# Two blocks of a transformer on one core: the mixers' gates as twelve-bit parts, each half unit a group

## The reference

```
def token_mix(x, w_in, ...):
    (sgu_u, sgu_v, ret_q, ret_k, ret_v, ret_g, pool_in,
     c_q, c_kv, k_rope, gate_logits) = _split(x @ w_in, IN_SIZES)
    ys = (sgu_mixer(...), retention_mixer(...), pool_mixer(...), mla_mixer(...))
    gates = jax.nn.sigmoid(gate_logits).reshape(bsz, seq, N_BRANCH, dm)
    merged = gates[:, :, 0] * (ys[0] @ w_branch[0])
    for n in range(1, N_BRANCH):
        merged = merged + gates[:, :, n] * (ys[n] @ w_branch[n])
    return merged @ w_out

for i in range(DEPTH):
    x = layer_norm(ALPHA * x + 0.5 * swiglu(x, ffn1_up[i], ffn1_down[i]), ...)
    x = layer_norm(ALPHA * x + token_mix(x, w_in[i], ...), ...)
    ple = jax.nn.sigmoid(x @ w_ple_gate[i]) * (p[i] @ w_ple[i])
    x = layer_norm(ALPHA * x + 0.5 * swiglu(x, ffn2_up[i], ffn2_down[i]) + ple, ...)
```

## Time and profile before

| | us |
|---|---|
| runs shown: median (of 3) | 2652.66 |
| lowest, highest | 2650.13, 2652.67 |
| profiled execution, its own time | 2655.03 |
| its span on the core | 2653.3 |
| gate stage of layer 1: first gate unit to first merge product | 277.55 to 411.34, 133.8 |
| the same in layer 2 | 987.28 to 1121.08, 133.8 |

### The profile page before, as it was taken

The page is one execution under the profiler, slowest core; times in us unless marked ns, Lnnn a source line. Parts: engine busy times, 40 slices in busy tenths (PEclk is TensorE's granted clock), DMA queues, the critical chain, the costliest instruction groups (busy, mean ns, idle before and its releaser), DMA issues.

```text
span 2653.3 us, 37978 instructions
## 1 busy us (share of the span) xinstructions
PE 2622.0 (99%) x15353; PEld 1913.9 (72%) x15353; DVE 1117.3 (42%) x1589; ACT 676.8 (26%) x1202; POOL 73.5 (3%) x95
## 2 busy tenths in 40 slices
PE   9999999999999999999999999999999999999998
PEld 9989888999999998899989888843333333333333
DVE  6866424686586563157832143321212212112212
ACT  4414220442243142213412043021212121112111
POOL 0010200000000120000001000000000000000000
PEclk9999999999999999999999999999999999999999
DMA  6685334456655843334562644699999999999999
GB/s 233 212 283 187 110 134 153 143 174 229 215 190 190 291 153 127 127 143 159 177 213 90 229 149 158 263 370 426 427 427 428 428 427 428 428 427 428 428 427 400
DMA packets 265652, 705.31 MB, mean 266 GB/s; under 512 B 13124, under 2 KB 155408, under 8 KB 215760
## 3 DMA queue, kind: packets, MB, share of 16 engines
q1 hardware_dynamic: 253520, 663.66, 64.8%
q0 software_dynamic: 9856, 36.41, 3.9%
q10 hardware_dynamic: 2176, 3.83, 0.4%
HBM read 699.61 MB, written 6.60 MB: 266 GB/s over the span
## 4 chain that ended last, share of the span: by engine, by line
PE 84%; DMA 8%; SPq 6%; DVE 1%; issue 1%; ACT 0%; DVEq 0%; ACTq 0%
PE acc L993 12%; PE acc L1090 11%; PE acc L1712 10%; PE acc L1047 6%; PE mix L1051 6%; PE acc L1049 6%; PE acc L1727 5%; SPq L875 4%; PE acc L1532 4%; PE mix L1041 4%; DMA big<-in_w 3%; PE acc L1019 3%; PE acc L1324 2%; SPq L878 2%; PE mix L1700 2%; PE acc L1585 2%
## 5 line engine op out<-in xcount | busy, mean ns | idle before, releaser
L1047 PE MATMUL acc<-branch_parts,area_parts 128*128 128x256 f32 x1176 | 343.9, 292 | 0.2
L1051 PE MATMUL mix<-big_parts,zz_parts 128*128 128x256 f32 x1176 | 332.8, 283 | 0.0
L1049 PE MATMUL acc<-area_parts,ring_parts 128*128 128x256 f32 x1176 | 332.4, 283 | 0.0
L1090 PE MATMUL acc<-big,ring 128*128 128x256 f32 (+1 forms) x1408 | 269.7, 353 | 0.0
L1090 PEld LDWEIGHTS acc<-big,ring 128*128 128x128 f32 x1408 | 241.1, 190 | 28.3 <-issue 0.8
L3027 DVE COPY zz<-acc 128x512 f32<-128x512 f32 x32 | 22.1, 692 | 546.4 <-PE acc L1712 546.4
L1047 PEld LDWEIGHTS acc<-branch_parts,area_parts 128*128 128x128 f32 x1176 | 225.0, 191 | 9.5 <-DVE zz_parts L2369 1.0
L1049 PEld LDWEIGHTS acc<-area_parts,ring_parts 128*128 128x128 f32 x1176 | 225.1, 191 | 0.2
L1051 PEld LDWEIGHTS mix<-big_parts,zz_parts 128*128 128x128 f32 x1176 | 225.0, 191 | 0.0
L993 PE MATMUL acc<-x,ring 128*128 128x256 f32 x1024 | 224.3, 380 | 0.0
L993 PEld LDWEIGHTS acc<-x,ring 128*128 128x128 f32 x1024 | 193.8, 190 | 26.7 <-issue 0.3
(11 more groups left out here) (522 smaller groups left out, 3841.6 us busy)
## 6 DMA issues: line engine op xcount, KB each, us to landing
ring<-in_ffn_up SPq DMA_DIRECT2D x86, 1024.0 KB, 5.0
big<-in_w SPq DMA_DIRECT2D x79, 1024.0 KB, 25.7
ring<-in_w SPq DMA_DIRECT2D x76, 1024.0 KB, 26.0
ring<-in_w_in SPq DMA_DIRECT2D x72, 1024.0 KB, 7.0
area<-in_w SPq DMA_DIRECT2D x57, 1024.0 KB, 26.4
spare<-in_w SPq DMA_DIRECT2D x38, 1024.0 KB, 25.7
area<-in_w_ada POOLq DMA_DIRECT2D x24, 1024.0 KB, 8.5
ring<-in_ffn_down SPq DMA_DIRECT2D x28, 768.0 KB, 4.7
```

The lines of the kernel that those rows point to most:

```text
L1047: pe.matmul(abank(a, b)[:, ts], wg[:, b, k, c * P:c * P + P], xg[:, k, :], start=c == 0 and k == 0, stop=False, skip_group_check=True)
L1049: pe.matmul(abank(a, b)[:, ts], wl[:, k, c0:c0 + P], xl[:, k, :], start=False, stop=k == K - 1, skip_group_check=True)
L1051: mm = pe.matmul(kbank(a, b)[:, ts], wk[:, b, k, c * P:c * P + P], xk[:, k, :], start=False, stop=k == K - 1, skip_group_check=True)
L1090: mm = pe.matmul(outs[c], w[:, k, c * P:c * P + P], rhs(kk), start=opens[c] and kk == 0, stop=kk == FC - 1, skip_group_check=not all(opens))
```

## The change

All eight gate units are now in parts. TensorE's list has `gate_product` for each in the place of `product` and of the last `split_product`: for each half unit (256 columns) a group of its own, whose two `acc` banks hold the g and l products (bank 0) and the K sum with the two plain chunks (bank 1). So the gates no longer use `mix`, and there are 8 more groups in a layer. ScalarE has `gate_sum` (copy the K sum to the gate's place in `big`, then `upper` for the same half of the next unit) and `gate` (sigmoid in place) per half; VectorE has `gate_join` (add the other bank, free the pair, then `lower` for the same half of the next unit).
The parts of x stay in `res` and `tn` up to the last gate unit; for this P transposed (`pT`) goes to `area`, and the weights' parts to the upper end of `area` and, for the last units, to places there that the steps are done with. The rotation of retention's q and k moves from step 0 (`m_stats`) to step 4 (`m_values`), with its VectorE work. The merge gets waits for the sigmoids of units 6 and 7. Counts of the semaphores follow.

```
+        gate_wg, gate_wk = (area_parts[:, c:c + IN].rearrange("p (b k c) -> p b k c", b=2, c=256) for c in (AREA + 2 * T, 5632))
+        def weight_parts(s, n):
+            if s < 2 or n < 4:
+                return PARTS[s][1:3]
+            return gate_wg, (PARTS[2][2] if n < 9 else gate_wk)
+        def gate_group(g, b):
+            return G_GATE + 2 * g + b
...
+            def gate_product(L, g):
+                r, n = GATE + g, 4 + g
...
+                unit_landed(pe, L, r)
+                for b in range(2):
+                    a = gate_group(g, b)
+                    group_open(pe, L, a)
+                    for c in range(2):
+                        c0 = (2 * b + c) * P
+                        for k in range(K, DC):
+                            pe.matmul(abank(a, 1)[:, c * T:c * T + T], w[:, k, c0:c0 + P], x[:, k, :], ...)
+                    pe.wait_ge(k_ready, half_parts(L, 2, n, b))
+                    for c in range(2):
+                        for k in range(K):
+                            pe.matmul(abank(a, 0)[:, ts], wg[:, b, k, c * P:c * P + P], xg[:, k, :], ...)
+                            ml = pe.matmul(abank(a, 0)[:, ts], wl[:, k, c0:c0 + P], xl[:, k, :], ...)
+                            mk = pe.matmul(abank(a, 1)[:, ts], wk[:, b, k, c * P:c * P + P], xk[:, k, :], ...)
+                    ml.then_inc(acc_done, 1)
+                    mk.then_inc(acc_done, 1)
...
                 for n in range(8):
-                    if n:
-                        product(L, GATE + n, G_GATE + n, xs, cols)
-                    else:
-                        split_product(L, 2, 4)
+                    gate_product(L, n)
                     steps[n](L)
...
-            def gate(L, n):
-                a = G_GATE + n
-                for b in range(2):
-                    bank_done(act, L, a, b)
-                    g = act.activation(big[:, 4 * n + 2 * b:4 * n + 2 * b + 2, :],
-                                       abank(a, b).rearrange("p (c t) -> p c t", c=2), ACT.Sigmoid)
-                g.then_inc(acc_free[a % 2], 1)
+            def gate_sum(L, g, b):
+                bank_done(act, L, gate_group(g, b), 1)
+                copy(gate_place(g, b), abank(gate_group(g, b), 1)...).then_inc(k_summed, 1)
+                if g < 7:
+                    upper(L, 2, 5 + g, b)
+            def gate(L, g, b):
+                act.wait_ge(a_joined, 38 * L + 11 + 2 * g + b + 1)
+                return act.activation(gate_place(g, b), gate_place(g, b), ACT.Sigmoid)
...
+            def gate_join(L, g, b):
+                a = gate_group(g, b)
+                bank_done(v, L, a, 1)
+                v.wait_ge(k_summed, sums_made(L, 2) + 6 + 2 * g + b + 1)
+                v.scalar_tensor_tensor(out=gate_place(g, b), in0=pair(abank(a, 0)), scalar=1.0 + 1.0 / STEP, in1=gate_place(g, b),
+                                       op0=ALU.mult, op1=ALU.add).then_inc(acc_free[a % 2], 1)
+                v.drain().then_inc(a_joined, 1)
+                if g < 7:
+                    lower(L, 2, 5 + g, b)
...
                 def merge(n, halves=(0, 1)):
                     br = ORDER[n]
+                    if n in (0, 2):
+                        v.wait_ge(silu_ready, 24 * L + (12, 13)[n // 2])
```

More of the change, by code:

```diff
@@ L235, in mixed_blocks @@
         tables = sb("tables", [P, 2048])
-        area_parts = over("area_parts", [P, 3, SPLIT, 256])
+        area_parts = over("area_parts", [P, WHOLE])
         area = sb("area", [P, WHOLE])
@@ L264, in mixed_blocks @@
         vz = carve(2, 2, T)
+        pT = shaped(area[:, 512:2048], (3, 512))
         vn = carve(2, T)
@@ L835, in _ @@
                 for n in range(8):
-                    banks(L, 2 * (G_PROJ + 3 + n) if n < 2 else 2 * (G_GATE + n - 1))
+                    banks(L, 2 * (G_PROJ + 3 + n) if n < 2 else 2 * gate_group(n - 1, 0))
                     square(L, w_in, GATE + n, MAIN + UC * n)
@@ L1210, in m_values @@
                 pe.wait_ge(rv_ready, L + 1)
+                pe.wait_ge(proj_qk, L + 1)
+                pe.matmul(mix[:, 1, :], const("rot_ret"), rq.rearrange("p c t -> p (c t)"), start=True, stop=True)
+                pe.matmul(mix[:, 2, :], const("rot_ret"), rk.rearrange("p c t -> p (c t)"), start=True, stop=True)
                 for b in range(NB):
@@ L1987, in _ @@
                 act.activation(ckvs, ckv, ACT.Square).then_inc(squares, 1)
-                for b in range(2):
-                    k_sum(4, b, big[:, 2 * b:2 * b + 2, :])
-                for b in range(2):
-                    act.wait_ge(a_joined, 24 * L + 11 + b + 1)
-                    act.activation(big[:, 2 * b:2 * b + 2, :], big[:, 2 * b:2 * b + 2, :], ACT.Sigmoid)
+                gate_sum(L, 0, 0)
+                gate_sum(L, 0, 1)
+                gate(L, 0, 0)
+                gate(L, 0, 1)
                 act.wait_ge(s0_var, L + 1)
                 act.activation(ml_std, ml_std, ACT.Sqrt).then_inc(s0_std, 1)
-                gate(L, 1)
+                gate_sum(L, 1, 0)
+                gate_sum(L, 1, 1)
+                gate(L, 1, 0)
                 act.wait_ge(s1_done, L + 1)
@@ L2002, in _ @@
                 c.then_inc(kv_ready, 1)
-                gate(L, 2)
+                gate(L, 1, 1)
+                gate_sum(L, 2, 0)
+                gate_sum(L, 2, 1)
+                gate(L, 2, 0)
                 act.wait_ge(s2_tr, L + 1)
                 copy(vtm.rearrange("p b c s -> p (b c s)"), mix[:, 3, :]).then_inc(vtm_ready, 1)
-                gate(L, 3)
+                gate(L, 2, 1)
+                gate_sum(L, 3, 0)
+                gate_sum(L, 3, 1)
+                gate(L, 3, 0)
+                gate(L, 3, 1)
+                gate_sum(L, 4, 0)
                 act.wait_ge(mx_ready, L + 1)
@@ L2015, in _ @@
                 e.then_inc(exp_done, 1)
-                gate(L, 4)
+                gate_sum(L, 4, 1)
+                gate(L, 4, 0)
                 act.wait_ge(s4_done, L + 1)
@@ L2019, in _ @@
                 copy(mvt.rearrange("p b h s -> p (b h s)"), mix[:, 0, :]).then_inc(vt_ready, 1)
-                gate(L, 5)
+                gate(L, 4, 1)
+                gate_sum(L, 5, 0)
+                gate_sum(L, 5, 1)
+                gate(L, 5, 0)
                 act.wait_ge(s5_pt, L + 1)
                 copy(pT, mix[:, 0:3, :]).then_inc(pT_ready, 1)
-                gate(L, 6)
-                gate(L, 7)
+                gate(L, 5, 1)
+                gate_sum(L, 6, 0)
+                gate_sum(L, 6, 1)
+                gate(L, 6, 0)
+                gate(L, 6, 1).then_inc(silu_ready, 1)
+                gate_sum(L, 7, 0)
+                gate_sum(L, 7, 1)
+                gate(L, 7, 0)
+                gate(L, 7, 1).then_inc(silu_ready, 1)
                 act.wait_ge(yc_ready, L + 1)
@@ L2284, in _ @@
             v.drain().then_inc(tab_ready, 1)
+            pair = lambda a: a.rearrange("p (c t) -> p c t", c=2)
             cos, sin, mcos, msin = (rope[:, n, :] for n in range(4))
@@ L2502, in layer_norm @@
                 scaled(3)
-            pair = lambda a: a.rearrange("p (c t) -> p c t", c=2)
             def modulation():
@@ L2570, in _ @@
                 v.tensor_copy(kpe[64:96, :], abank(a, 0)[64:96, 0:T]).then_inc(acc_free[a % 2], 1)
-                join(L, 2, 4, 0, big[:, 0:2, :]).then_inc(a_joined, 1)
-                join(L, 2, 4, 1, big[:, 2:4, :]).then_inc(free(4), 1)
-                v.drain().then_inc(a_joined, 1)
+                gate_join(L, 0, 0)
+                gate_join(L, 0, 1)
                 v.wait_ge(s0_done, L + 1)
@@ L2585, in _ @@
                 v.drain().then_inc(s0_var, 1)
-                for t, bank in ((rq, 1), (rk, 2)):
-                    tt(rt, pair(mix[:, bank, :]), bc(sin, 2), ALU.mult)
-                    tt(t, t, bc(cos, 2), ALU.mult)
-                    v.drain()
-                    tt(t, t, rt, ALU.add)
-                    v.drain()
-                v.drain().then_inc(ret_roped, 1)
+                tt(vn, vz[:, :, 0, :], bc(lnmu[:, :], 2), ALU.subtract)
                 v.wait_ge(s0_std, L + 1)
-                v.reciprocal(ml_std, ml_std)
+                v.reciprocal(ml_std[:, 1:3, :], ml_std[:, 1:3, :])
                 v.drain()
@@ L2650, in _ @@
                 tt(s1, s1, sums[:, 4:8].unsqueeze(2).to_broadcast([P, 4, T]), ALU.mult).then_inc(prob_ready, 1)
+                gate_join(L, 4, 1)
+                v.wait_ge(s4_done, L + 1)
+                for t, bank in ((rq, 1), (rk, 2)):
+                    tt(rt, pair(mix[:, bank, :]), bc(sin, 2), ALU.mult)
+                    tt(t, t, bc(cos, 2), ALU.mult)
+                    v.drain()
+                    tt(t, t, rt, ALU.add)
+                    v.drain()
+                v.drain().then_inc(ret_roped, 1)
+                gate_join(L, 5, 0)
+                gate_join(L, 5, 1)
                 v.wait_ge(s5_pool, L + 1)
```

73 lines of the change are left out of this document (49 added, 24 removed).

## The result

| | before | after |
|---|---|---|
| median of the runs compared | 2652.66 (4 runs) | 2625.82 (4 runs) |
| lowest, highest | 2650.13, 2653.25 | 2624.13, 2627.23 |
| profiled execution, its span | 2655.03, 2653.3 | 2624.61, 2622.9 |
| gate stage, layer 1 | 133.79 | 276.34 to 397.34, 121.00 |
| gate stage, layer 2 | 133.8 | 973.19 to 1094.18, 120.99 |

All in us. The ratio of the times is 0.9898, with a 95% interval of 0.9885 to 0.9910: the changed kernel is 26.8 us faster. The forecast was 24.0.

The account below looks back on a forecast made before the run. TensorE, busy for 99% of the span, was taken to bound the kernel. The gates' matmuls save 24.0 us and all other terms are 0, so the median goes from 2652.66 to 2628.7 us, range 2623 to 2639.

Parts of the forecast that it names:

- The bound: Whole kernel: TensorE, busy for 99% of the span, sets the time; VectorE and ScalarE are covered in the gate stage.
- Matmuls of the gates: Gate units 1 to 7, two layers: leaving the plain form takes 24.0 us off TensorE, bounds 20 and 25 us.
- Waits and groups: Gate half units: two groups for one and six waits for three per unit cost 0, at most 0.2 us.
- The sentence on the change of form: Gate units: changing form costs a little back, the first record in parts taking 0.47 us and the next 0.28.
- What TensorE waits for: Gate stage: added VectorE and ScalarE work is never late, cost 0; tightest at the latents, ready 1.2 us early.
- The loads: Gate weights fetched by DMA: at worst 1.5 us late for ScalarE, inside 2.7 us of cover, cost 0.
- What moves: Rotations of q and k to step 4, P transposed to `area`, merge waits for the last sigmoids: 0 net.
- Rival A: VectorE late at the latents and near units 5 and 6: 8 of 24 us given back, 2637 us; chance 0.12.
- Rival B: VectorE bounds the gate stage: gain gone at 5.5 us a lower pair, 2667 us at 6; chance 0.04.
- Rival C: Gate records in parts come every 0.108 us, not 0.120: 12 us more gain, 2617 us; chance 0.02.
- Rival D: TensorE pays 0.4 us a gate unit for changing between forms and groups: 2634 us; chance 0.10.
- What would show it: Trace signs: gate units 12.1 to 12.3 us, stage 121.8, VectorE busy some 90 us, no TensorE idle at tight places.

Follow-up runs that it names:

- The two doses: Changed kernel with an unread reciprocal (128x128, then 128x256) and a drain added on VectorE before each lower part of the gates: 2632.55 and 2650.45 us.
- the second dose: Changed kernel with an unread 128x256 reciprocal (1.75 us) and a drain added on VectorE before each lower part of the gates: 2650.45 us, ratio 0.9994.

## Why the prediction was right, and where its size was off

**The bound.** TensorE alone sets the time in this stage: it is busy in all of it before and after, and what was taken from it came off the end. The plain form under the new groups restores the old time. The median of 2625.8 lies in the range of 2623 to 2639, but just under the 2626 to 2632 that carried the chance of 0.70; that of the repeated runs, 2627.7, lies in both.

**Matmuls of the gates, the mis-sized term.** The sum was 14 x (13.88 - 12.17) = 24.0 us, and "I take 12.17, since it was measured in the same place". Units 1 to 7 take 12.07 on average, which makes 14 x 1.81 = 25.4, and unit 0 itself lost 0.08, twice: 25.6 us. Nearly all of it is the pace: the records follow each other every 0.1185 us and not 0.120, 72 x 0.0012 = 0.09 us a unit, and the run with the upper parts of units 0 and 1 put back gives the old pace there. The rest nearly cancels. The first half after a step was paid at 6.13 us, 0.1 more than the second half; in units 1, 2, 3 and 6 it takes 6.00 like the others. But the second halves of units 6 and 7 take 6.08, and unit 7's first half goes at the slow pace. The upper bound of 25 us, from two second halves of 6.04, was thus passed too. The move of the upper parts stood in the diff, and I gave it no price because nothing in the trace of before had one.
The other 1.2 us of the 26.8 lie within the scatter of the medians, which the repeated run gives as 2 us.
On the rule of the Trainium skill (TensorE: Matmul & The Clock Gate, Back-to-back issue gap), 109 ns at 256 columns for isolated matmuls: the trace after does not show it either. It shows 118.5 ns in most halves of the gates and 119.7 elsewhere, and the time by that rule, 2618 us, lies 6 us below the lowest run.

**Waits and groups at 0.** Right: the plain form with all of them runs at the time of before. The sentence on the change of form was wrong. What the first record costs more, the plain ones before the next change of form give back.

**What TensorE waits for.** The walk through VectorE's list held in each place where it was made. Latents: cover 1.2 forecast, 1.3 found. Unit 5's second half: 3 us forecast and found. Unit 6's first half: 2.7 forecast, 2.5 found. These are the ends of the parts in VectorE's timeline and the records that need them in TensorE's:

```profile
357.15 1.76 DVE L2432 SCALAR_TENSOR_TENSOR area_parts<-area_parts,ring_parts 128x1536 fp32r<-128x1536 f32 x1
361.86 0.47 PE L1091 MATMUL acc<-tn_parts,area_parts 128*128 128x256 f32 x1
...
365.92 1.76 DVE L2432 SCALAR_TENSOR_TENSOR area_parts<-area_parts,ring_parts 128x1536 fp32r<-128x1536 f32 x1
370.04 0.47 PE L1091 MATMUL acc<-tn_parts,area_parts 128*128 128x256 f32 x1
```

The two doses then broke these covers in the order given, save that the latents, with the least of it, were reached late: only one pair of a lower part stands ahead of them there, so a dose is paid once, where units 5 and 6 carry many. A tight place is found by cover over the work piled up ahead of it, not by cover alone.

**The loads.** Right: ScalarE waited 0.5 us, once.

**What moves.** Right, and shown by its undoing: without the move of the rotations the latents come 1.13 us late.

**Rival A, small waits,** did not come: no wait of TensorE in the stage, and the gates' lower parts took 1.76 us each, with GpSimd's last operation over by 280.0 and the first of them at 284.6. **Rival B, VectorE as the bound,** did not come, and the second dose shows that it stood about 1.8 us per lower part away. **Rival C, records at 0.108 us,** had a grain in it: the pace did change, for another reason and by a tenth of that. **Rival D, 0.4 us more a unit,** fell; the form costs nothing over its records.

**What would show it.** The units were to take 12.1 to 12.3 us and the stage 121.8: they take 11.99 to 12.23 (five of the seven under 12.1), and 121.0. VectorE's 90 us are 92.4.

## What to carry to other kernels

When one engine is busy all the time, count its records and their pace in the form that is already in the program, and walk the other engines' lists to each place where it will ask: both numbers came out of the old trace here to 0.1 us in 12. Then look for what the edit moves besides: an operand's place had a price, small and not to be seen before. Put a dose of idle work on the engine that fills the cover; it tells how far the next bound is and where it comes first, which a kernel without waits can't show. And where a stretch that the change does not touch differs between two profiles, ask for its granted clock before anything else.

## What was not expected of the hardware

**The place of an operand.** The pace of records in parts has two values, near 0.1185 and near 0.1198 us. With the weights' upper parts in `big` every half went at the slower one; with them at the upper end of `area`, one number changed, most halves went at the faster one. Some did not, and what tells these apart is open.

**A wait costs more than its idle time in the view.** The stage grew by 1.36 us for a wait shown with 1.13 (the rotations back), by 1.04 for one of 0.75 (plain chunks first), by 2.95 for two of 2.42 together, by 11.2 for eight of 8.7: some 0.3 us more for each. More than half of that is how the records are drawn. A record in parts is drawn 0.28 us long and a plain one 0.38, while the next one starts after 0.1185 or 0.2158 us. The idle time counts from the drawn end of the last record, so 0.16 us of each delay lies under it. The rest is the start: after the wait of 1.06 us the first record in parts is followed after 0.23 us, and without a wait it starts 0.03 after the last plain one and is followed after 0.31. That makes 1.06 + 0.38 + 0.23 - 0.03 - 0.31 = 1.33 us, and the half grew by 7.32 - 6.00 = 1.32. So a sum of idle times read from the view is too low by this for each wait.

**The rest of the program.** The part of the program that the change does not touch is not the same length in every profiled execution. From the second layer's first merge product to the end of the span it took 1532.2 us before, 1528.7 after, and between 1526.6 and 1531.6 in the ten experiments, without regard to the kernel. That is 3.5 of the 30.4 us between the two profiled executions, more than all by which the forecast missed. Most of it is the clock of TensorE in the routing to the experts. TensorE's timeline and the windows from its start there to the experts' products, before:

```profile
1710.18 3.31 PE L1615 MATMUL mix<-consts_sb,tn 128*128 128x1 f32 x16
1713.35 1.95 PE L1624 MATMUL mix<-consts_sb,x 128*128 128x128 f32 x8
...
1710.18:1740.90 30.72, 30.02 (x158) 24.65 (x159) 7.18 (x35) 8.52 (x24) 0.00 (x0) 0.83 0.88 370
```

and after:

```profile
1683.30 1.93 PE L1654 MATMUL mix<-consts_sb,tn 128*128 128x1 f32 x16
1685.08 1.19 PE L1663 MATMUL mix<-consts_sb,x 128*128 128x128 f32 x8
...
1683.30:1711.17 27.87, 26.98 (x158) 21.67 (x159) 7.17 (x35) 8.53 (x24) 0.00 (x0) 0.94 0.97 410
```

The windows have their columns as in the earlier trace rows. The same 24 records take 2.1 us less after, and the whole stretch 2.85: its mean granted clock is 0.94 after and 0.83 before. From 1710.5 to 1717.2 us before, and from 1686.0 to 1689.3 after, it is 0.50, the lower level of 1.2 GHz. All twelve profiles go by this clock and not by the kernel. Two have 0.94 and 27.9 us, five have 0.88 and 29.1 to 29.5, five have 0.83 to 0.85 and 30.4 to 30.8, the repeated run of the changed kernel among these last. Ahead of the routing TensorE did the same before and after: 3.5 us of matmuls of 32 columns, without idle time. Why the clock then is low for longer in one execution than in another is open. The single runs go the same way: of the 89 runs of the changed kernel, the experiments and the kernel before beside them, the 21 with a mean granted clock of 0.999 lie on average 1.2 us under the mean of their kernel's set, the 21 with 0.997 lie 0.7 over it. The other 0.7 us of the 3.5 lie with the experts. For a change of one per cent it means: compare the stage that was changed from trace to trace, and the whole only by medians.
